# The end of a differential attention: filler products in one wait, short products in two groups, two output columns moved forward

## The chip, the cores and the metric

One core of a Trainium2 chip (trn2) runs the whole program in one launch. The time is device microseconds of an execution, the median of several. Everything below is about one stretch of some 60 us out of 1887.

## The reference

The program computes two transformer blocks over 512 tokens of width 1024. The stretch at hand is the last attention, `diff_attention`: 8 heads, each the difference of two softmaxes, then a norm over each head's 128 values, then the output projection, added to the residual.

```python
s = einsum('bhitd,bhisd->bhits', q, k) * scale      # two score maps per head
s = s + bias; s = where(dist >= 0, s, -inf)
p = softmax(s, axis=-1)
a = p[:, :, 0] - lam * p[:, :, 1]
o = einsum('bhts,bhsd->bhtd', a, v)                 # 8 heads x 128 values per token
o = rms_norm_2(o, subln) * (1.0 - lambda_init)      # norm over the 128 values of one head
x = x + o.reshape(B, S, V_WIDTH) @ w_o              # 1024 -> 1024
```

## The kernel before, in words

Every dense product is made of three TensorE products of rounded halves: high by high, low by high, high by low (lines 475 to 477). ScalarE rounds a weight unit to its high half (`w_hi`, line 1126), VectorE subtracts to get the low half (`w_lo`, line 1693), and SyncE's queue loads the next raw unit when VectorE has finished with the slot. There are two weight slots.

The attention is a software pipeline of items. Item n stands for head n//4 and query block n%4, so there are 32 items, and each engine has its own function `diff_item(n)` that is called for n = 0, 1, 2, ... in order. Each engine works strictly down its own list; semaphores (`a3[...]`) join them. In call n TensorE does, in this order: `turn(n-4)`, transposes of the finished probabilities against `ident` (line 1028); `scores(n)`, six products over 64 rows (line 1017); now and then `head_sums`, the sums of squares of one finished head (line 972, a column of ones as the moving operand); `heads_turned` and `head_spread`, which turn four heads' factors into rows and spread them over 128 partitions with products over only 4 rows (lines 980, 990, 991); half of a query/key panel (up to call 25); and in odd calls `weigh(n-6)`, probabilities by values. VectorE does in call n: the low half of the turned probabilities (line 2370) for n-5, `inverse(n-2)`, `least(n)` (line 2345, which waits for the scores), `probs(n-3)` (line 2361, for which the turn waits), weight low halves (line 1693), and `head_normed` and `head_lo` for heads whose factors are there (lines 2421 and 2426). ScalarE does the exponentials, the high halves and the copy of a finished head out of bank 6 (line 1610), and `head_square` (line 1651).

The output projection is cut in two. Heads 0 to 3 give the "early" part: 8 columns (j = 0 to 7) of 128 output channels, each a chain of 12 products of 512 columns (`early_column`), in banks 7 and 3 by turns, each added to `x` by VectorE (line 1756) before the bank is used again. Two columns share a weight unit, and a unit's slot is free after the second. Heads 4 to 7 give the "bo" part behind all of that (`into_residual`), whose first column goes head by head and waits for each head's low half (`a3["out_lo"]`).

In the kernel before, early columns 0 to 3 stand in calls 30, 31, 33 and 35, and columns 4 to 7 behind the loop, between the last sums of squares, the turned factors and the four spreads of heads 4 to 7. `output_column(0)` waits for all four heads 0 to 3.

Of the kernel before, what the change touches and what calls it, by code (L numbers as in the profile page):

```python
# [122 lines left out]
def bass_two_blocks(nc, weights, x_cols, mem_cols, positions, params, consts, dil_table, head_rows, alibi_table, head_picks,  # L123
# [26 lines left out]
    with ctx:  # L150
# [156 lines left out]
            return [half.rearrange("p (j b n) -> p j b n", b=2, n=P) for half in halves]  # L307

        BO_EARLY = 4 * N_DIFF - 2
        COLUMN_ITEMS = (BO_EARLY, BO_EARLY + 1, BO_EARLY + 3, BO_EARLY + 5)  # L310

        def head_squares(h):

# [79 lines left out]
        OPENING_BANKS = (0, 1, 4, 5, 6)  # L393
        OPENING = len(OPENING_BANKS)
        IDLE_PRODUCTS = 13

        ROWS = {"mix": 0, "first": 1, "a": 2, "kv": 3}

# [73 lines left out]
        def _(pe):  # L472
# [494 lines left out]
            def head_sums(h):  # L967

                pe.wait_ge(a3["sq"], h + 1)
                for b in range(TB):  # L970
                    i = 16 * (h // 4) + TB * b + h % 4
                    mm = nc.tensor.matmul(ps[:, 2, i:i + 1], head_squares(h)[:, b, :], ones[:, 0:1], start=True, stop=True)  # L972
                mm.then_inc(a3["summed"], 1)
# [9 lines left out]
            def head_spread(h, bank):  # L983

                g = h // 4
                if h % 4 == 0:
                    pe.wait_ge(a3["rms"], 4 * g + 5)
                hi, lo = token_rows(g)
                pick = head_picks_r[:, h % 4 * P:(h % 4 + 1) * P]
                nc.tensor.matmul(ps[:, bank, :], pick, hi, start=True, stop=False)  # L990
                nc.tensor.matmul(ps[:, bank, :], pick, lo, start=False, stop=True).then_inc(a3["spread"], 1)

            def output_column(j):

                if j == 0:
                    pe.wait_ge(a3["out_lo"], 4)
                if j < 2:
                    pe.wait_ge(a3["normed"], 3 + j)
                else:
                    pe.wait_ge(early["added"], ADDED["bo_early"] + j - 1)  # L1000
                early_column("bo_early", j, 3 if j % 2 else 7, da["xb_hi"], da["xb_lo"])

            def diff_item(n):
                def scores(n):
                    s, b = n // TB, n % TB
                    if b == 0:
                        pe.wait_ge(a3["staged"], 2 * (s + 1))
                    if n:
                        pe.wait_ge(a3["least"], 2 * n)
                    w = P * (b + 1)  # L1010
                    qh, ql, kh, kl = (at3[f"{p}{s % 2}"] for p in ("qhi", "qlo", "khi", "klo"))
                    block_ = slice(b * P, (b + 1) * P)

                    for k, (q_, k_) in enumerate(((qh, kh), (qh, kl), (ql, kh))):
                        for h in range(2):
                            rows = slice(HD * h, HD * h + HD)
                            mm = nc.tensor.matmul(ps[:, h, 0:w], q_[rows, block_], k_[rows, 0:w],  # L1017
                                                  start=k == 0, stop=k == 2)
                            if k == 2:
                                mm.then_inc(a3["scores"], 1)  # L1020

                def turn(n):
                    b = n % TB
                    pe.wait_ge(a3["probs"], n + 1)
                    if n >= 2:
                        pe.wait_ge(a3["pt"], n - 1)
                    for j in range(b + 1):
                        mm = nc.tensor.transpose(ps[:, 4 + n % 2, j * P:(j + 1) * P],  # L1028
                                                 at3["e"][:, 2 * (n % DIFF_SLOTS), j * P:(j + 1) * P], ident)
                    mm.then_inc(a3["turned"], 1)  # L1030

                def weigh(n):
                    s, pair = n // TB, n % TB // 2
                    pe.wait_ge(a3["pt"], n + 1)
                    if pair == 0:
                        pe.wait_ge(a3["v_staged"], s + 1)
                        pe.wait_ge(a3["out"], s + 1)
                    vh, vl = at3[f"vhi{s % 2}"], at3[f"vlo{s % 2}"]
                    hi, lo = turned_pair(s, pair)
                    last = 2 * pair + 1  # L1040
                    for j in range(last + 1):
                        cols = slice(j * P, (j + 1) * P)
                        one = j == last
                        mm = product(ps[:, 6, (2 * pair + one) * P:2 * (pair + 1) * P].rearrange("p (b n) -> p b n", n=P), vh[:, cols], vl[:, cols],
                                     hi[:, j, one:, :], lo[:, j, one:, :], j == 0, j == last)
                    mm.then_inc(a3["pv"], 1)

                if live(n - 4):
                    turn(n - 4)
                if live(n):  # L1050
                    scores(n)
                if n >= 12 and n % TB == 0 and n // TB - 3 < N_DIFF - 1:
                    head_sums(n // TB - 3)
                if n == 25:
                    heads_turned(0, 3)
                if n == 26:
                    pe.wait_ge(kv["qk"], 2 * N_DIFF)
                    head_spread(0, 7)
                if n == 27:
                    head_spread(1, 3)  # L1060
                    pe.wait_ge(a3["normed"], 1)
                    head_spread(2, 7)
                if n == 28:
                    pe.wait_ge(a3["normed"], 2)
                    head_spread(3, 3)
                p = EARLY_PANELS + n // 2
                if p < 2 * N_DIFF:

                    if n % 2 == 0 and n:
                        pe.wait_ge(kv["qk"], p)  # L1070
                    half_panel(qk0 + p, ps[:, 7, :], *qk_input(p), n % 2)
                if n in COLUMN_ITEMS:
                    output_column(COLUMN_ITEMS.index(n))
                if live(n - 6) and n % 2:
                    weigh(n - 6)

            diff_items(diff_item, 6)
            pe.wait_ge(a3["least"], 8 * N_DIFF)
            output_column(4)
            head_sums(N_DIFF - 1)  # L1080
            output_column(5)
            heads_turned(1, 0)
            output_column(6)
            for h, bank in ((4, 1), (5, 2), (6, 0), (7, 1)):
                if h == 7:
                    pe.wait_ge(a3["normed"], 5)
                head_spread(h, bank)
            output_column(7)
            into_residual("bo", KC, 4, da["xb_hi"], da["xb_lo"], a3["out_lo"], lambda k: k + 1,
                          {0: (a3["pt"], 4 * N_DIFF), 2: (a3["out"], N_DIFF + 1), 3: (early["added"], ADDED["bo_early"] + KC - 1),  # L1090
                           4: (a3["normed"], N_DIFF), 7: (early["added"], ADDED["bo_early"] + KC)}, LAST)
# [26 lines left out]
        def _(act):  # L1118
            def split(u, i=None):

                if u >= N_UNITS:
                    return
                act.wait_ge(w_loaded[u % 2], at(16 * (u // 2 + 1), i, 16))
                if u >= 2:
                    act.wait_ge(used, at(u - 1, i, 2))
                nc.scalar.activation(w_hi[:, u % 2, :], w_raw[:, u % 2, :], ACT.Copy).then_inc(w_hi_ready, 1)  # L1126
# [455 lines left out]
            def diff_item(n):  # L1582
# [56 lines left out]
                    head_hi(2)  # L1639
                if n == 29:  # L1640
                    head_hi(3)
                for f in (0, 1):
                    if n == COLUMN_ITEMS[2 * f + 1] + 1:
                        split(FIRST["bo_early"] + 2 + f)

            def head_square(h):
                act.wait_ge(a3["v_staged"], 1 + h % 2)
# [39 lines left out]
        def _(dve):  # L1687
# [644 lines left out]
            def diff_item(n):  # L2332
# [60 lines left out]
                    head_normed(2, 7)  # L2393
                    head_lo(0)
                if n == 28:
                    head_normed(3, 3)
                    head_lo(1)
                    head_lo(2)
                if n == 29:
                    head_lo(3)  # L2400
                if n - 1 in COLUMN_ITEMS:
                    output_column(COLUMN_ITEMS.index(n - 1))
                for f in (0, 1):
                    if n == COLUMN_ITEMS[2 * f + 1] + 1:
                        split(FIRST["bo_early"] + 2 + f)

            def heads_inverse(g):

# [10 lines left out]
            def head_normed(h, bank):  # L2419
                dve.wait_ge(a3["spread"], 5 * (h // 4) + h % 4 + 2)  # L2420
                nc.vector.scalar_tensor_tensor(out=da["o"][:, h, :], in0=da["o"][:, h, :], scalar=subln[:, 0:1],
                                               in1=ps[:, bank, :], op0=ALU.mult, op1=ALU.mult).then_inc(a3["normed"], 1)
# [7 lines left out]
                early_sum("bo_early", j, 3 if j % 2 else 7)  # L2430

            diff_items(diff_item, 5)
            output_column(4)
            heads_inverse(1)
            output_column(5)
            heads_lo(1)
# [2 lines left out]
            head_normed(4, 1)  # L2439
            head_normed(5, 2)  # L2440
            head_lo(4)
            head_normed(6, 0)
            head_lo(5)
            head_normed(7, 1)
            head_lo(6)
            output_column(7)
            head_lo(7)
            split(FIRST["bo"] + 1)
            dve.wait_ge(early["added"], ADDED["bo_early"] + KC)
# [309 lines left out]
```

## Time and profile before

| | us |
|---|---|
| median of 3 runs (1888.59, 1888.62, 1890.22) | 1888.62 |
| the profiled execution's own time | 1889.28 |
| its span, first to last instruction | 1887.4 |
| TensorE busy in that span | 1863.0 (99%) |
| VectorE busy | 1098.3 (58%) |
| ScalarE busy | 768.0 (41%) |

The span is what the trace shows; 1.9 us of the execution lie around it. The mean granted TensorE clock is 0.992 of full speed. The page's strip of 40 slices has the granted clock at 9 tenths or more in all but two slices (one in the attention's end, one at the end of the program). A stretch of the trace is read from the window view, which gives the busy time of each engine in it and the granted clock.

### The profile page before, as it was taken

Reading aid. Unit: us, or ns where it says so; the run is one execution under the profiler, and the core shown is the slowest. Engines: PE = TensorE matmul, PEld = TensorE weight load, DVE = VectorE, ACT = ScalarE, POOL = GpSimd, SP = SyncE. Lnnn points to the kernel's source line nnn. Section 1 sums busy time; section 2 is a strip of 40 time slices with the busy share of each in tenths; the row PEclk is TensorE's granted clock in tenths of the full one; section 3 lists DMA queues with packets and bytes.
Section 4 is the critical chain, followed back from the end, with each engine's and each line's share of the span. In section 5 each row is a group of like instructions: output and inputs, shape, how many; then the busy total and the mean of one; then the engine's idle time right before and its main releaser. Section 6 shows DMA issues by size and latency. Waiting matters only on the chain.

```text
span 1887.4 us, 24931 instructions
## 1 busy us (share of the span) xinstructions
PE 1863.0 (99%) x8782; PEld 1526.1 (81%) x8782; DVE 1098.3 (58%) x1577; ACT 768.0 (41%) x1182; POOL 261.1 (14%) x206
## 2 busy tenths in 40 slices
PE   9999999999999999999999999999999999999998
PEld 7877888788888888888888888888787888888886
DVE  6867976676777524677544442254888654444223
ACT  4226654355545413563333222144557433323212
POOL 4803320020000001301100000021643110000001
PEclk9999999999999999999999999999998999999998
DMA  5232322122222332222222322332211222222232
GB/s 181 92 109 73 103 97 76 56 90 100 90 99 89 123 100 89 93 87 90 98 97 95 98 95 96 100 104 96 68 56 34 68 95 96 98 97 95 97 100 78
DMA packets 62837, 174.48 MB, mean 92 GB/s; under 512 B 5428, under 2 KB 23988, under 8 KB 62648
## 3 DMA queue, kind: packets, MB, share of 16 engines
q1 hardware_dynamic: 61424, 169.50, 26.8%
q10 hardware_dynamic: 1016, 2.92, 0.5%
q0 software_dynamic: 336, 1.25, 0.2%
q8 instruction: 39, 0.64, 0.1%
q14 instruction: 22, 0.18, 0.0%
HBM read 171.54 MB, written 2.10 MB: 92 GB/s over the span
## 4 chain that ended last, share of the span: by engine, by line
PE 91%; DVE 6%; ACT 1%; issue 1%; DMA 0%; POOL 0%; SPq 0%; POOLq 0%; DVEq 0%; ACTq 0%
PE ps L475 29%; PE ps L477 29%; PE ps L476 29%; DVE w_lo L1693 1%; PE ps L1017 1%; PE ps L1028 1%; DMA x<-in_x_cols 0%; PE ps L972 0%; DVE at_e L1928 0%; DVE sg_z L2225 0%; ACT w_hi L1126 0%; PE ps L503 0%; DVE sg_t L2221 0%; PE ps L685 0%; DVE sg_u L2230 0%
## 5 line engine op out<-in xcount | busy, mean ns | idle before, releaser
L1693 DVE TENSOR_TENSOR w_lo<-w_raw,w_hi 128x1024 fp32r<-128x1024 f32 x314 | 405.5, 1291 | 456.4 <-ACT w_hi L1126 455.9
L475 PE MATMUL ps<-xg_hi,w_hi 128*128 128x512 f32 (+1 forms) x1448 | 564.7, 390 | 4.2 <-DVE w_lo L1765 1.9
L476 PE MATMUL ps<-xg_lo,w_hi 128*128 128x512 f32 (+1 forms) x1448 | 557.6, 385 | 0.0
L477 PE MATMUL ps<-xg_hi,w_lo 128*128 128x512 f32 (+1 forms) x1448 | 557.3, 385 | 0.0
L1126 ACT ACTIVATE w_hi<-w_raw 128x1024 fp32r<-128x1024 f32 x314 | 330.5, 1052 | 533.7 <-PE ps L477 529.7
L475 PEld LDWEIGHTS ps<-xg_hi,w_hi 128*128 128x128 f32 x1448 | 272.3, 188 | 70.9 <-DVE w_lo L1693 7.8
L477 PEld LDWEIGHTS ps<-xg_hi,w_lo 128*128 128x128 f32 x1448 | 272.4, 188 | 54.7
L476 PEld LDWEIGHTS ps<-xg_lo,w_hi 128*128 128x128 f32 x1448 | 272.6, 188 | 53.3 <-issue 1.0
L475 PE MATMUL ps<-hid_hi,w_hi 128*128 (+1 forms) x528 | 205.5, 389 | 0.0
L477 PE MATMUL ps<-hid_hi,w_lo 128*128 (+1 forms) x528 | 205.4, 389 | 0.0
L476 PE MATMUL ps<-hid_lo,w_hi 128*128 (+1 forms) x528 | 205.4, 389 | 0.0
L2476 POOL COPY square_sum<-squares 128x512 f32<-128x512 f32 x7 | 4.8, 686 | 947.0 <-ACT squares L1141 946.0
L475 PEld LDWEIGHTS ps<-hid_hi,w_hi 128*128 128x128 f32 x528 | 99.1, 188 | 20.9 <-DVE w_lo L1693 0.4
L476 PEld LDWEIGHTS ps<-hid_lo,w_hi 128*128 128x128 f32 x528 | 99.1, 188 | 20.7
L477 PEld LDWEIGHTS ps<-hid_hi,w_lo 128*128 128x128 f32 x528 | 99.1, 188 | 20.4
L2479 POOL TENSOR_TENSOR square_sum<-square_sum,squares 128x512 f32<-128x512 f32 x49 | 78.3, 1597 | 61.3 <-ACT squares L1141 60.3
L475 PE MATMUL ps<-w_hi,xg_hi 128*128 128x512 f32 x192 | 77.4, 403 | 0.3 <-DVE w_lo L1693 0.3
L1714 DVE TENSOR_TENSOR conv_a<-ps,r_cols 128x512 f32<-128x512 f32 x44 | 30.4, 691 | 78.5 <-PE ps L477 78.5
L477 PE MATMUL ps<-w_hi,xg_lo 128*128 128x512 f32 x192 | 74.8, 390 | 0.0
L476 PE MATMUL ps<-w_lo,xg_hi 128*128 128x512 f32 x192 | 74.8, 390 | 0.0
L1543 ACT ACTIVATE gate<-conv_g 128x512 f32<-128x512 f32 x44 | 27.8, 632 | 109.0 <-DVE conv_g L1714 109.0
L1699 DVE SCALAR_TENSOR_TENSOR xg_lo<-x,par,xg_hi 128x512 fp32r<-128x512 f32 x56 | 60.7, 1098 | 6.7 <-ACT xg_hi L1191 6.6
(375 smaller groups left out, 2460.6 us busy)
## 6 DMA issues: line engine op xcount, KB each, us to landing
w_raw<-in_weights SPq DMA_DIRECT2D x315, 512.0 KB, 3.3
out_cols<-result SPq DMA_DIRECT2D x8, 256.0 KB, 2.2
x<-in_x_cols SPq DMA_DIRECT2D x2, 512.0 KB, 5.7
x<-in_x_cols SPq DMA_DIRECT2D x1, 1024.0 KB, 8.9
squares<-in_mem_cols ACTq DMA_DIRECT2D x1, 512.0 KB
sp_w<-in_spatial ACTq DMA_DIRECT2D x1, 512.0 KB
sp_b<-in_spatial_bias ACTq DMA_DIRECT2D x1, 512.0 KB
dil<-in_dil_table POOLq DMA_DIRECT2D x1, 448.0 KB, 4.8
```

The source lines that it names most:

```text
L475: nc.tensor.matmul(to, wh, xh, start=start, stop=False)
L476: nc.tensor.matmul(to, wh, xl, start=False, stop=False)
L477: return nc.tensor.matmul(to, wl, xh, start=False, stop=stop)
L1017: mm = nc.tensor.matmul(ps[:, h, 0:w], q_[rows, block_], k_[rows, 0:w], start=k == 0, stop=k == 2)
L1028: mm = nc.tensor.transpose(ps[:, 4 + n % 2, j * P:(j + 1) * P], at3["e"][:, 2 * (n % DIFF_SLOTS), j * P:(j + 1) * P], ident)
L1126: nc.scalar.activation(w_hi[:, u % 2, :], w_raw[:, u % 2, :], ACT.Copy).then_inc(w_hi_ready, 1)
L1543: nc.scalar.activation(ffn["gate"][:], ffn["tg"][:], ACT.Silu).then_inc(st["gated"], 1)
L1693: nc.vector.tensor_tensor(w_lo[:, u % 2, :], w_raw[:, u % 2, :], w_hi[:, u % 2, :].bitcast(F32), ALU.subtract).then_inc(w_ready, 1)
L1699: nc.vector.scalar_tensor_tensor(out=xg_lo[:, c, :], in0=x[:, c, :], scalar=column(gain, c), in1=xg_hi[:, c, :].bitcast(F32), op0=ALU.mult ...
L1714: return nc.vector.tensor_tensor(to, ps[:, bank, 0:cols], r_cols[:] if r is None else r, ALU.mult).then_inc(signal, 1)
L2476: nc.gpsimd.tensor_copy(sums[:], squares[:, 0, :]).then_inc(summed, 1)
L2479: nc.gpsimd.tensor_tensor(sums[:], sums[:], squares[:, c % 2, :], ALU.add).then_inc(summed, 1)
```

## The change

On TensorE, `turn(23)` (IDLE_TURN) gets eight products of `ident` by `ident` between its two waits: after the wait for the bank, ahead of the wait for the probabilities. Columns 0 and 1 of the early part leave calls 30 and 31; `first_columns(h)` does the share of head h in both columns at once (six products), in call 28 (h = 0), 29 (h = 1 and 2) and 30 (h = 3). Columns 2, 3 and 4 go to calls 32, 33 and 35, so one column fewer stands behind the loop. `head_spread(3)` goes to bank 2 and no longer waits for `normed` 2; `head_sums(4)`, which uses bank 2 too, goes from call 28 to call 30. Behind the loop the four spreads are done as 4 and 5, then column 7, then 6 and 7. ScalarE and VectorE follow: columns 0 and 1 are both added in call 31, weight units 2 and 3 of the early part are split in calls 31 and 34 (before: 32 and 36), column 4 is added in call 36, and column 7 ahead of `head_normed(6)`.

```diff
-        COLUMN_ITEMS = (BO_EARLY, BO_EARLY + 1, BO_EARLY + 3, BO_EARLY + 5)
+        COLUMN_ITEMS = (BO_EARLY + 2, BO_EARLY + 3, BO_EARLY + 5)
+        IDLE_TURN = 4 * N_DIFF - 9
+            def first_columns(h):
+                u = FIRST["bo_early"]
+                if h == 0:
+                    pe.wait_ge(w_ready, u + 1)
+                    pe.wait_ge(a3["normed"], 3)
+                pe.wait_ge(a3["out_lo"], h + 1)
+                for j in range(2):
+                    wh, wl = tile(u % 2, 2 * h + j)
+                    mm = product(ps[:, 3 if j else 7, :], wh, wl, da["xb_hi"][:, h, :], da["xb_lo"][:, h, :], h == 0, h == LAST - 1)
+                    if h == LAST - 1:
+                        mm.then_inc(used if j else early["first"], 1)
...
-                    pe.wait_ge(a3["probs"], n + 1)
                     if n >= 2:
                         pe.wait_ge(a3["pt"], n - 1)
+                    if n == IDLE_TURN:
+                        for _ in range(8):
+                            nc.tensor.matmul(ps[:, 4 + n % 2, 0:P], ident, ident, start=True, stop=True)
+                    pe.wait_ge(a3["probs"], n + 1)
...
-                if n >= 12 and n % TB == 0 and n // TB - 3 < N_DIFF - 1:
+                if n >= 12 and n % TB == 0 and n // TB - 3 < N_DIFF - 1 and n != 28:
                     head_sums(n // TB - 3)
+                if n == 30:
+                    pe.wait_ge(a3["normed"], 4)
+                    head_sums(4)
...
                 if n == 28:
-                    pe.wait_ge(a3["normed"], 2)
-                    head_spread(3, 3)
+                    head_spread(3, 2)
...
+                if n == 28:
+                    first_columns(0)
+                if n == 29:
+                    first_columns(1)
+                    first_columns(2)
+                if n == 30:
+                    first_columns(3)
 
             diff_items(diff_item, 6)
             pe.wait_ge(a3["least"], 8 * N_DIFF)
-            output_column(4)
             head_sums(N_DIFF - 1)
             output_column(5)
             heads_turned(1, 0)
             output_column(6)
-            for h, bank in ((4, 1), (5, 2), (6, 0), (7, 1)):
-                if h == 7:
-                    pe.wait_ge(a3["normed"], 5)
-                head_spread(h, bank)
+            head_spread(4, 1)
+            head_spread(5, 2)
             output_column(7)
+            head_spread(6, 0)
+            pe.wait_ge(a3["normed"], 5)
+            head_spread(7, 1)
```

## Rows read from the trace of the kernel before

**Rows 1.** The page: busy us of each engine and share of the span.
```profile
PE 1863.0 (99%) x8782; PEld 1526.1 (81%) x8782; DVE 1098.3 (58%) x1577; ACT 768.0 (41%) x1182; POOL 261.1 (14%) x206
```

**Rows 2.** Windows: length; PE, PEld, DVE, ACT, POOL busy (count); clock; DMA; GB/s.
```profile
1439.42:1453.06 13.64, 13.64 (x58) 9.93 (x54) 12.56 (x36) 8.20 (x21) 0.75 (x2) 0.50 0.12 40
1487.20:1490.62 3.42, 3.42 (x10) 2.65 (x9) 2.07 (x4) 1.26 (x2) 0.00 (x0) 0.50 0.00 0
1453.06:1487.20 34.14, 34.14 (x191) 27.68 (x192) 20.41 (x42) 17.16 (x35) 1.72 (x2) 1.00 0.15 47
```

**Rows 3.** Timeline of TensorE, calls 26 to 29: start, us, operation, count [idle before].
```profile
1434.80 0.52 PE L1028 MATMUL ps<-con,at_e 128*128 128x128 f32 x3
1435.97 0.49 PE L990 MATMUL ps<-xg_hi 4*128 4x512 f32 x1
1438.47 0.66 PE L1028 MATMUL ps<-con,at_e 128*128 128x128 f32 x4 [1.78 <-DVE at_e L2361]
1446.84 0.79 PE L990 MATMUL ps<-xg_hi 4*128 4x512 f32 x1
1447.98 0.69 PE L1028 MATMUL ps<-con,at_e 128*128 128x128 f32 x2
1449.54 0.58 PE L475 MATMUL ps<-at_pt_hi,at_v_hi 128*128 128x256 f32 x1
```

**Rows 4.** Timeline of VectorE, calls 27 to 31.
```profile
1443.22 0.35 DVE L2361 SCALAR_TENSOR_TENSOR at_e<-at_e,at_inv 128x128 f32<-128x128 f32 x1
1444.80 0.68 DVE L2426 TENSOR_TENSOR xb_lo<-da_o,xb_hi 128x512 fp32r<-128x512 f32 x1
1446.77 0.48 DVE L2361 SCALAR_TENSOR_TENSOR at_e<-at_e,at_inv 128x256 f32<-128x256 f32 x1
1459.45 0.35 DVE L2361 SCALAR_TENSOR_TENSOR at_e<-at_e,at_inv 128x128 f32<-128x128 f32 x1
```

**Rows 5.** Timeline of TensorE, calls 31 to 36 and the six steps behind the loop.
```profile
1456.58 0.60 PE L1028 MATMUL ps<-con,at_e 128*128 128x128 f32 x4
1461.52 0.29 PE L1028 MATMUL ps<-con,at_e 128*128 128x128 f32 x1
1471.91 0.36 PE L475 MATMUL ps<-at_pt_hi,at_v_hi 128*128 128x256 f32 x1
1473.35 0.44 PE L475 MATMUL ps<-xb_hi,w_hi 128*128 128x512 f32 x1
1476.16 0.95 PE L972 MATMUL ps<-con,da_v 128*128 128x1 f32 x8
1483.86 0.49 PE L990 MATMUL ps<-xg_hi 4*128 4x512 f32 x1
1486.08 0.50 PE L475 MATMUL ps<-xb_hi,w_hi 128*128 128x512 f32 x1
1488.27 0.63 PE L476 MATMUL ps<-xb_lo,w_hi 128*128 128x512 f32 x1
1488.69 0.63 PE L477 MATMUL ps<-xb_hi,w_lo 128*128 128x512 f32 x1
1490.40 0.49 PE L475 MATMUL ps<-xb_hi,w_hi 128*128 128x512 f32 x1
```

**Rows 6.** Timeline of ScalarE behind the last weigh.
```profile
1474.22 0.63 ACT L1651 ACTIVATE da_v<-da_o 128x512 f32<-128x512 f32 x1
```

**Rows 7.** Timeline of TensorE at the start; two windows of it.
```profile
1.19 5.36 PE L594 MATMUL ps<-squares 128*128 128x128 f32 x26 [1.19 <-DVE squares L1759]
5.80:6.55 0.75, 0.75 (x7) 0.55 (x5) 0.00 (x0) 0.72 (x1) 0.00 (x0) 1.00 0.95 382
9.26:12.68 3.42, 3.42 (x9) 2.35 (x9) 2.22 (x4) 2.29 (x4) 0.92 (x2) 0.51 1.00 379
```

**Rows 8.** Two thin windows of the first attention.
```profile
162.90:166.40 3.50, 2.12 (x17) 1.84 (x18) 1.97 (x3) 3.45 (x10) 2.22 (x4) 1.00 0.00 0
197.00:200.50 3.50, 2.60 (x28) 2.18 (x27) 3.43 (x10) 1.30 (x4) 0.00 (x0) 1.00 0.27 90
```

More of the change, by code:

```diff
@@ L991, in head_spread @@
                 nc.tensor.matmul(ps[:, bank, :], pick, lo, start=False, stop=True).then_inc(a3["spread"], 1)
-            def output_column(j):
[L995 to L1000, printed above, removed]
+            def first_columns(h):
[9 more added lines that the diff above has]
+                        mm.then_inc(used if j else early["first"], 1)
+            def output_column(j):
+                pe.wait_ge(early["added"], ADDED["bo_early"] + j - 1)
                 early_column("bo_early", j, 3 if j % 2 else 7, da["xb_hi"], da["xb_lo"])
@@ L1072, in diff_item @@
                 if n in COLUMN_ITEMS:
-                    output_column(COLUMN_ITEMS.index(n))
+                    output_column(2 + COLUMN_ITEMS.index(n))
                 if live(n - 6) and n % 2:
                     weigh(n - 6)
+                if n == 28:
[5 more added lines that the diff above has]
+                    first_columns(3)
             diff_items(diff_item, 6)
             pe.wait_ge(a3["least"], 8 * N_DIFF)
-            output_column(4)
             head_sums(N_DIFF - 1)
@@ L1641, in diff_item @@
                     head_hi(3)
-                for f in (0, 1):
-                    if n == COLUMN_ITEMS[2 * f + 1] + 1:
-                        split(FIRST["bo_early"] + 2 + f)
+                if n == BO_EARLY + 1:
+                    split(FIRST["bo_early"] + 2)
+                if n == COLUMN_ITEMS[1] + 1:
+                    split(FIRST["bo_early"] + 3)
             def head_square(h):
@@ L2395, in diff_item @@
                 if n == 28:
-                    head_normed(3, 3)
+                    head_normed(3, 2)
                     head_lo(1)
@@ L2400, in diff_item @@
                     head_lo(3)
+                if n == BO_EARLY + 1:
+                    output_column(0)
+                    output_column(1)
                 if n - 1 in COLUMN_ITEMS:
[L2402 to L2405, printed above, removed]
+                    output_column(2 + COLUMN_ITEMS.index(n - 1))
+                if n == BO_EARLY + 1:
+                    split(FIRST["bo_early"] + 2)
+                if n == COLUMN_ITEMS[1] + 1:
+                    split(FIRST["bo_early"] + 3)
             def heads_inverse(g):
@@ L2432, in _ @@
             diff_items(diff_item, 5)
-            output_column(4)
             heads_inverse(1)
@@ L2441, in _ @@
             head_lo(4)
+            head_lo(5)
+            output_column(7)
             head_normed(6, 0)
-            head_lo(5)
             head_normed(7, 1)
             head_lo(6)
-            output_column(7)
             head_lo(7)
```

## The prediction, made before the changed kernel was seen

> **What bounds the kernel now.** I read the page first: TensorE is busy for 1863.0 us, 99% of the span [rows 1]. So an edit pays only by work taken off TensorE, by a gap closed, or by TensorE running at its higher clock. No product is taken away here; one gap is filled. The window view shows the third: in 13.64 us of the stretch the granted clock is 0.50, that is 1.2 GHz, and again in 3.42 us behind it; the 34.14 us between are at 1.00, 2.4 GHz [rows 2]. The timeline of TensorE shows what goes ahead of each fall: a spread over 4 rows, 1.78 us in which it waits for VectorE's `probs(23)`, four transposes and products over 64 rows [rows 3]; and, in the second place, the four spreads over 4 rows, 1483.86 to 1486.08 [rows 5]. These are the two places that the change touches. The third view is VectorE in the same 13.64 us: 12.56 us busy [rows 2]. The low clock is therefore not all that TensorE pays there. Even at full clock it would stand behind VectorE.
>
> The sum is made against the profiled execution, 1889.28 us (span 1887.4 and 1.9 around it), and is then moved to the median of 1888.62, which lies 0.66 lower.
>
> **The identity products.** Eight products of an f32 operand. The thirteen f32 products of the same size at the program's start have 26 records, so each is two passes and eight are 16. Those 26 took 5.36 us, 0.21 each; the last seven, in 0.75 us, 0.11 to 0.13 each [rows 7]. Sixteen cost 1.7 to 2.0 us at the fast pitch and 3.4 at the slow one. The wait is 1.78 us, so `turn(23)` starts 0 to 0.3 us later, or 1.6 later at the slow pitch. Either is hidden: the next thing TensorE needs from VectorE is `probs(24)`, which ends at 1443.22 + 0.35 = 1443.57 [rows 4], and VectorE comes to it through its own queue (the weight unit, one norm, the two maps of call 27). Cost taken: 0. Without that cover it would be 0.3.
>
> **Do they hold the clock?** Through the wait, I think yes. But what follows is thin as well, and stays thin at full clock: scores over 64 rows, spread 1, a wait for `normed` 1, spread 2, six products of `weigh(21)`, a wait until 1443.57 for `probs(24)`, one transpose, small scores, spread 3, and then a wait for `out_lo` 1, which is written at 1444.80 + 0.68 = 1445.48 [rows 4]. The changed call 28 has dense work only from there on. So I take it that the fall is put off, not gone: half rate from about 1442.8, and the high clock back at about 1449.7, behind the first six column products. The two ends for this are no low stretch at all, and one that lasts to 1453.06 as before.
>
> **Calls 28 to 31, walked through.** VectorE's order does not change up to `probs(25)`, whose end is 1446.77 + 0.48 = 1447.25 [rows 4]. In the middle case:
> - `turn(24)` and `scores(28)`, then spread 3 at half rate, done at about 1445.7. Spread 3 comes some 2 us earlier than before (it began at 1446.84 and took 1.0 [rows 3]) because the sums of head 4 are gone from ahead of it.
> - Six column products at 0.425 (1488.27 to 1488.69 is one at half rate [rows 5]), 2.55: 1448.3.
> - `turn(25)` and `scores(29)` at half rate, 1447.98 to 1449.54, 1.56 [rows 3]: 1449.85.
> - `weigh(23)`: twelve products at full rate, 1471.91 to 1473.35, 1.44 [rows 5]: 1451.3.
> - Heads 1 and 2, twelve products, 2.81 (column 4: 1473.35 to 1476.16 [rows 5]): 1454.1.
> - `turn(26)` and `scores(30)`, as 1434.80 to 1435.97, 1.17 [rows 3]: 1455.3; the sums of head 4, about 0.9 (0.95 for such a group at 1476.16 [rows 5]): 1456.2; head 3, 1.4: 1457.6.
> - `turn(27)` to the end of `probs(28)`: before, 1456.58 [rows 5] to 1459.45 + 0.35 [rows 4], 3.2. It is a chain over scores, VectorE's two minima and `probs`, and TensorE has only the scores and `weigh(25)` to put beside it, 2.1 us; so it now stands idle for 1.1. `turn(28)` at 1460.8, and before at 1461.52 [rows 5].
>
> This part gives -0.7 us: the move fills what VectorE made thin, but one column of cover (2.8) is gone from call 31. Of what is queued behind the waiting `first_columns` on TensorE only `turn(25)` matters, and that has its own wait until 1447.25. The units' splits at calls 31 and 34 come earlier than their users (columns 4 to 7); SyncE's loads follow those splits and have several us in hand: 0.
>
> With no low stretch at all the same walk gives `turn(28)` at about 1459.0, -2.5. With a low one up to 1453.06 it adds 1.6: +0.9.
>
> **Behind call 31.** Columns 2, 3 and 4 are now inside the loop, the same work in another order: 0. But before, column 4 (2.8 us) lay between `weigh(31)` and the sums of head 7. Those sums need head 7 copied and squared, and the square ended at 1474.22 + 0.63 = 1474.85 [rows 6], 1.5 us behind the end of `weigh(31)` at 1473.35 [rows 5]. Nothing covers that chain now: +1.5.
>
> **Two groups of spreads.** Column 7 took 1486.08 to 1490.40, 4.32, against 2.81 at full rate [rows 5]. With 1.1 us of spreads, a dense column and 1.1 us again I expect no fall: -1.5. The low end of this is 0 (it falls all the same).
>
> **VectorE behind column 7.** It adds column 7 (0.7), norms heads 6 and 7, and takes both low halves, one at a time with 0.6 to 0.7 each. The low half of head 6 is there some 2.8 us behind column 7; TensorE comes to it after two spreads (1.1) and the six products of heads 4 and 5 (1.4), so it waits for 0.3: +0.3. Bounds 0 and 1.
>
> **Sum.** -0.7 + 1.5 - 1.5 + 0.3 = -0.4 us, 1888.9 for the profiled execution and 1888.2 for the median.
>
> **A rule weighed.** Rows first: the clock is at 0.50 for 13.64 + 3.42 = 17.06 us [rows 2]. The Trainium skill, "TensorE: Matmul & The Clock Gate", section "Terms", puts the penalty of throttled time at that time by (1 - K/N), half of it here. By that the change could win 8.5 us, where I count 2.5 + 1.5 at best before the new gaps.
>
> **Rivals.**
> - *The clock's half comes back whole.* 13.64 / 2 + 1.5 = 8.3 us, less the new waits of 1.5 and 0.3 and a part of the 1.1: -6, 1882.6. For it: TensorE had no gap in the 13.64 us. Against it: VectorE is 92% busy there, and `probs(24)` and `probs(25)` don't come earlier. Chance 0.12. The rule of the skill above is this case.
> - *No low stretch, but VectorE as counted.* -2.5 + 1.5 - 1.5 + 0.3 = -2.2, 1886.4. For it: windows of the first attention in which TensorE was busy for only 2.12 and 2.60 of 3.50 us kept 1.00 [rows 8]. Against it: they held dense products, and the thin stretch here holds few. Chance 0.14.
> - *The other side: the new gap behind `weigh(31)` brings the clock down.* There 1.5 us of idle and 0.9 of products with one column follow 1.4 us of dense ones. The rows decide neither way: a window with about as little, 197.00 to 200.50, kept 1.00 [rows 8], and at the program's start, less than 3 us behind the last pass of the f32 products, the clock was 0.51 [rows 7]. If it falls as the second stretch of before did, 3.42 us at half rate under the sums and column 5 cost 1.7: sum +1.3, 1889.9. It decides from the clock in column 5. Chance 0.25.
> - *The identity products don't help:* the low stretch lasts to about 1453 as before. Sum -0.4 + 1.6 = +1.2, 1889.8. Chance 0.13; together with the one before, 1891.5 and more, within these two.
> - *The forecast,* one shorter low stretch and none later, 0.36.
>
> **How the numbers follow.** A measurement of this kernel can tell about 0.2%, 3.8 us, from no change. Faster by more: the first rival, and a part of the second if VectorE gives more than I count, 0.16. Slower by more needs both falls and a third in the gap of call 32, 0.07. Within: 0.77. The forecast is 1888.2; alone its range is 1887.2 to 1889.2. The whole range takes in the second rival and both falls, and leaves most of the first outside: 1884.8 to 1891.4.
>
> **What would show it.** The gap before `turn(23)` filled with 16 passes of `ident` (0.12 each) and `turn(23)` within 0.3 us of its place. Granted clock 1.00 to about 1442.8 and 0.50 for some 7 us. A wait of TensorE for VectorE's line 2361 in call 32 of about 1.1 us, one for ScalarE's `head_square` of 1.5 us before the last sums. Column 7 in 2.8 us. I am wrong if VectorE's busy time in calls 27 to 31 turns out to have been stretched by TensorE's low clock, or if the clock falls where I have it high.

## The result: 4.1 us slower, and the profile after

The changed kernel takes 1892.91 us (median of 17; 1892.05 to 1894.45), the kernel before 1888.83 (median of 17; 1888.35 to 1890.22). The ratio is 1.0020, 95% interval [1.0013, 1.0027]. The forecast was 1888.2 with a range up to 1891.4, so the time lies outside it, on the slow side.

The profiled execution took 1892.56 us, span 1890.7. First the page: engine, busy us, share, instructions. Against [rows 1] TensorE has 16 more instructions, 3.0 us more busy time and 2.3 us more of weight loads (PEld). The other engines stay within 0.3 us.

```profile
PE 1866.0 (99%) x8798; PEld 1528.4 (81%) x8798; DVE 1098.2 (58%) x1577; ACT 768.3 (41%) x1182; POOL 261.3 (14%) x206
```

Then the windows with a granted clock below 1.00 in the attention's end (columns as in [rows 2]):

```profile
1443.54:1450.26 6.72, 6.72 (x27) 4.71 (x24) 6.12 (x21) 5.20 (x15) 0.00 (x0) 0.50 0.01 2
1477.60:1484.41 6.81, 6.81 (x21) 4.95 (x21) 0.79 (x2) 1.42 (x3) 0.00 (x0) 0.50 0.00 0
1484.41:1495.03 10.62, 10.45 (x45) 7.05 (x43) 8.19 (x13) 3.83 (x7) 0.00 (x0) 1.00 0.16 51
```

The first low stretch has gone from 13.64 us to 6.72. The one of 3.42 under column 7 is gone. But there is a new one of 6.81 us, in a place where the kernel before had 1.00. The timeline of TensorE (start, us, operation, count, [idle before <- releaser]) shows what lies around both:

```profile
1435.24 0.49 PE L991 MATMUL ps<-xg_hi 4*128 4x512 f32 x1
1435.90 2.05 PE L1037 MATMUL ps<-con 128*128 128x128 f32 x16
1437.79 0.62 PE L1040 MATMUL ps<-con,at_e 128*128 128x128 f32 x4
...
1442.99 0.30 PE L1040 MATMUL ps<-con,at_e 128*128 128x128 f32 x1 [0.80 <-DVE at_e L2383]
...
1445.01 0.80 PE L476 MATMUL ps<-xb_hi,w_hi 128*128 128x512 f32 x1
...
1447.73 0.63 PE L1040 MATMUL ps<-con,at_e 128*128 128x128 f32 x2
...
1449.23 0.58 PE L476 MATMUL ps<-at_pt_hi,at_v_hi 128*128 128x256 f32 x1
...
1460.83 0.30 PE L1040 MATMUL ps<-con,at_e 128*128 128x128 f32 x1 [1.03 <-DVE at_e L2383]
...
1477.11 1.40 PE L973 MATMUL ps<-con,da_v 128*128 128x1 f32 x8 [1.49 <-ACT da_v L1673]
1478.37 0.77 PE L476 MATMUL ps<-xb_hi,w_hi 128*128 128x512 f32 x1
1478.94 0.63 PE L477 MATMUL ps<-xb_lo,w_hi 128*128 128x512 f32 x1
...
1483.77 1.34 PE L981 MATMUL ps<-con,lam_in 128*4 128x128 f32 x8
1485.04 0.50 PE L476 MATMUL ps<-xb_hi,w_hi 128*128 128x512 f32 x1
...
1489.12 0.50 PE L476 MATMUL ps<-xb_hi,w_hi 128*128 128x512 f32 x1
...
1493.19 0.50 PE L476 MATMUL ps<-xb_hi,w_hi 128*128 128x512 f32 x1
...
1495.03 0.50 PE L476 MATMUL ps<-xb_hi,w_hi 128*128 128x512 f32 x1 [0.17 <-DVE xb_lo L2452]
```

In the kernel before, column 6 starts here:

```profile
1480.89 0.50 PE L475 MATMUL ps<-xb_hi,w_hi 128*128 128x512 f32 x1
```

The two executions are laid on each other at spread 0 (1435.24 here, 1435.97 in [rows 3]), so 0.73 is added to the times here. That 0.73 is also why the two profiled executions differ by only 3.28 us (1892.56 less 1889.28): up to spread 0 both kernels do the same work, and this execution happened to be there earlier. Then `turn(28)` is at 1461.56 against 1461.52 [rows 5]: nothing won. The last sums are at 1477.84 against 1476.16: 1.7 lost. Column 6 is at 1485.77 against 1480.89: 4.9 lost. The "bo" part starts at 1493.92 (1493.19 above) against 1490.40 [rows 5]: 3.5 lost, and 0.3 more where its third head waits. The whole loss arises between `weigh(31)` and column 6: 1.7 us of wait and 3.2 us of half clock, of which the two groups of spreads give 1.4 back.

### The profile page after: what moved, and what is told of

The parts are those of the page before. It is cut to its first block, busy times and chain, and to the rows that moved or that the text cites. A ratio compares the mean times of both kernels' runs of the same rounds, so it can differ in the third digit from the quotient of the medians.

```text
span 1890.7 us, 24964 instructions
## 1 busy us (share of the span) xinstructions
PE 1866.0 (99%) x8798; PEld 1528.4 (81%) x8798; DVE 1098.2 (58%) x1577; ACT 768.3 (41%) x1182; POOL 261.3 (14%) x206
## 4 chain that ended last, share of the span: by engine, by line
PE 91%; DVE 6%; issue 1%; ACT 1%; DMA 0%; POOL 0%; SPq 0%; POOLq 0%; DVEq 0%; ACTq 0%
PE ps L476 29%; PE ps L477 29%; PE ps L478 29%; DVE w_lo L1715 1%; PE ps L1026 1%; PE ps L1040 0%; DMA x<-in_x_cols 0%; PE ps L973 0%; PE ps L686 0%; DVE at_e L1950 0%; DVE sg_z L2247 0%; PE ps L504 0%; DVE sg_t L2243 0%; PE ps L695 0%; DVE sg_u L2252 0%
```

## The experiments

All times are medians, beside runs of the kernel before on the same chip (1889.13 for the first four, 1889.3 for the next four, 1889.18 for the last four). In the result it was 1888.83, so the same kernel differs by 0.3 to 0.5 us from one set of runs to the next, and a difference between kernels of different sets is not known better than that. The two numbers in brackets behind a ratio are its 95% interval.

**1. Column 4 put back behind the loop.**

```diff
-        COLUMN_ITEMS = (BO_EARLY + 2, BO_EARLY + 3, BO_EARLY + 5)
+        COLUMN_ITEMS = (BO_EARLY + 2, BO_EARLY + 3)
...
+            output_column(4)
             head_sums(N_DIFF - 1)
```

VectorE adds column 4 behind the loop as well (left out above).

> The changed kernel with early column 4 put back behind the loop, between weigh(31) and the sums of head 7. Theory A (the loss sits in the uncovered chain behind weigh(31): 1.5 us of gap, and a low clock of 6.8 us under the sums, column 5 and the turned factors that costs 3.4): about 4.9 us less than the changed kernel, 1888.0, no wait before the last sums, clock 1.00 there. Theory B (the loss sits in calls 28 to 31, where the two columns are gathered head by head and call 31 has lost its cover): at most 0.5 us less, 1892.4 or more.

Measured 1892.4 (1890.82 to 1894.45), ratio to before 1.0017 [1.0008, 1.0026]. By its number this is theory B's result, but the trace doesn't put the loss in calls 28 to 31:

```profile
1469.46 0.95 PE L1040 MATMUL ps<-con,at_e 128*128 128x128 f32 x7
1472.15 1.05 PE L973 MATMUL ps<-con,da_v 128*128 128x1 f32 x8 [0.87 <-ACT da_v L1674]
1473.58 0.39 PE L476 MATMUL ps<-at_pt_hi,at_v_hi 128*128 128x256 f32 x1 [0.37 <-DVE at_pt_lo L2393]
```

and, its windows there:

```profile
1469.00:1475.10 6.10, 4.85 (x40) 4.43 (x40) 2.29 (x3) 2.93 (x5) 0.00 (x0) 1.00 0.22 73
1475.13:1478.54 3.41, 3.41 (x10) 2.64 (x10) 0.00 (x0) 2.51 (x3) 0.00 (x0) 0.50 0.06 20
```

The wait before the last sums is covered again, and two waits have opened in calls 36 and 37, where column 4 had been the cover; the clock falls behind them instead. My reading is that the two columns done early leave one too few for the waits behind call 31, wherever it is missing; theory A then had the mechanism and the wrong remedy, for its 1888.0 was missed by 4.4.

**2. The wait before the last sums filled.** Six products of `ident` by `ident` into bank 0, just ahead of `head_sums(N_DIFF - 1)`:

```diff
             pe.wait_ge(a3["least"], 8 * N_DIFF)
+            for _ in range(6):
+                nc.tensor.matmul(ps[:, 0, 0:P], ident, ident, start=True, stop=True)
             head_sums(N_DIFF - 1)
```

> The changed kernel with six more products of the identity (12 passes, about 1.45 us) in the gap before the sums of head 7; the gap itself stays. Theory A with the clock as its larger part: clock 1.00 in column 5, about 3.4 us less than the changed kernel, 1889.5. If the gap alone is the price: 1892.9, no change. If the identity's products don't count for the clock: 0.50 in column 5 all the same, and 1892.9 to 1893.1.

Measured 1889.88 (1889.32 to 1891.25), ratio 1.0005 [0.9996, 1.0014]: 3.0 us less than the changed kernel, although 12 instructions were added and TensorE still waits for head 7's squares. (Each taken against the kernel before of its own set, the difference is 3.3.) Its highest time, 1891.25, lies below the changed kernel's lowest, 1892.05. The timeline and one window:

```profile
1475.40 1.55 PE L1101 MATMUL ps<-con 128*128 128x128 f32 x12
1476.96 1.05 PE L973 MATMUL ps<-con,da_v 128*128 128x1 f32 x8
1477.88 0.48 PE L476 MATMUL ps<-xb_hi,w_hi 128*128 128x512 f32 x1
```

```profile
1476.00:1484.40 8.40, 8.39 (x48) 6.61 (x47) 2.76 (x4) 3.92 (x6) 0.00 (x0) 1.00 0.00 0
```

The "bo" part starts 54.64 us behind spread 0 here and 57.95 in the changed kernel, 3.3 apart. This is the cause of most of the loss, shown: the low clock behind the wait, not the wait. What is left above the kernel before, 0.75, agrees with the wait's 1.7, the two groups' -1.4 and the 0.3 of the third head.

**3. Without the products of the identity.** The loop of eight in `turn(23)` left out.

> The changed kernel without its eight products of the identity in turn(23). My walk: the clock falls some 3.4 us earlier, but TensorE stands behind VectorE's probs(24) and probs(25) there, so it costs 0 to 0.5 us: 1892.9 to 1893.4. Rival (the products hold the clock and that is worth what the low stretch costs): 1.7 us or more, 1894.6 and up. Third: they only delay turn(23), and without them it is up to 0.3 us faster.

Measured 1893.2 (1892.54 to 1894.95), 1.0023 [1.0014, 1.0033]: 0.3 more than the changed kernel, and equal to it (4.1 each) when each is taken against the kernel before of its own set. Both lie within my walk's 0 to 0.5. The first low stretch is 10.24 us long, from 1440.10, instead of 6.72, and that costs almost nothing: `turn(28)` is 25.64 us behind spread 0, in the changed kernel 25.59.

```profile
1440.10:1450.34 10.24, 9.89 (x34) 6.46 (x33) 9.16 (x28) 7.03 (x18) 0.00 (x0) 0.51 0.17 53
```

**4. The four spreads together again**, in the changed kernel: spreads 4, 5, 6, 7, then column 7, VectorE's order as before.

> The changed kernel with the four spreads of heads 4 to 7 together again, column 7 behind them and VectorE's order as before the change. If the grouping is worth what I gave it (1.5 us of column 7 at half rate, less 0.3 of waiting on VectorE): 1.2 us more, 1894.1, clock 0.50 in column 7. Rival (the fall there depends on what else is thin nearby and does not come every time): between -0.3 and 0, 1892.6 to 1892.9.

Measured 1893.82 (1890.57 to 1895.12), 1.0021 [1.0012, 1.0030], but the 11 times lie in two heaps, five from 1890.57 to 1891.62 and six from 1893.82 to 1895.12. The profiled execution is in the lower one, with 3.41 us at 0.50 behind the wait (1478.11 to 1481.52) where the changed kernel had 6.81. And its column 7 ran at 1.00, although the four spreads stood together before it:

```profile
1482.00:1496.00 14.00, 14.00 (x63) 10.32 (x63) 10.80 (x15) 5.46 (x8) 0.00 (x0) 1.00 0.14 43
```

The grouping is worth 0.6 to 0.9 here by the medians, below my 1.2. With two heaps that figure depends on how many executions fall into each, and which falls the upper heap has is not shown, since none of it was profiled.

**5. The grouping alone**, in the kernel before (the `for` over four spreads replaced by the order of the change, on VectorE too).

> The kernel before with only the grouping of the four spreads (4 and 5, column 7, 6 and 7, and VectorE's order with it). The grouping is worth what I predicted: clock 1.00 in column 7, -1.5 + 0.3 = -1.2 us, 1887.9. Rival: the fall there comes at another place or not in every execution, so that little is left: 1888.8 to 1889.4.

Measured 1888.97 (1887.87 to 1890.09), 0.9997 [0.9988, 1.0006]. Its trace has 1.00 throughout column 7 and "bo" starts 52.99 us behind spread 0 where the kernel before needed 54.43, 1.4 of the 1.5 I had predicted; by the medians only 0.3 is left. The number is the rival's. That the fall under column 7 is not in every execution of the kernel before is an inference: with the four spreads together, experiments 4 and 9 each have a trace without it.

**6. The columns' move alone**: the changed kernel without the eight products and with the spreads together.

> The changed kernel without the products of the identity and with the spreads together: what is left is the gathering of columns 0 and 1 in calls 28 to 30 and one column fewer behind the loop. Theory (the columns' move is what costs; the rest is small): 4 to 5.5 us more than before, 1893.2 to 1894.6, with the 1.5 us wait before the last sums and a low clock behind it. Rival (the parts hurt only together): below 1891.

Measured 1894.19 (1891.64 to 1895.30), 1.0024 [1.0015, 1.0033], 4.9 us above before, as the theory had it. Its trace has the wait of 1.49 us before the last sums and this behind it:

```profile
1477.50:1484.32 6.82, 6.82 (x21) 5.20 (x21) 0.25 (x1) 1.25 (x2) 0.00 (x0) 0.50 0.00 0
```

The move is the part that costs; the other two soften it by 0.8 (each against before of its own set) to 1.3.

**7. Every wait filled**, in the changed kernel: 3 products ahead of `pe.wait_ge(a3["normed"], 1)`, in `turn` this, 3 ahead of the first `out_lo` wait, and the six of experiment 2.

```diff
-                    if n == IDLE_TURN:
-                        for _ in range(8):
+                    if n in (23, 24, 25, 28):
+                        for _ in range({23: 8, 24: 3, 25: 1, 28: 4}[n]):
```

The other three places (left out above) are loops like experiment 2's.

> The changed kernel with products of the identity in every wait of TensorE from call 27 on: 8 in turn(23) as there, 3 before spread 2, 3 and 1 and 4 in turn(24), turn(25) and turn(28), 3 before the first column products, 6 before the last sums. Two theories on what the low clock of calls 28 and 29 is worth. VectorE sets the order there: the clock stays at 1.00, turn(25) still starts only behind probs(25), and it is 2 to 2.5 us faster than with the last sums' gap filled alone (1889.9): 1887.5. The clock's half comes back whole: 3.4 us (half of 6.9) faster, 1886.5 or less. If the filler takes time itself: 1889.9 or more.

Measured 1888.7 (1887.43 to 1890.49), 0.9996 [0.9987, 1.0005]: 1.2 us less than experiment 2, where I had expected 2 to 2.5. In the traces the "bo" part comes 2.1 earlier (52.54 us behind spread 0 against 54.64), so the medians give back less than this one execution shows. One window over calls 27 to 31:

```profile
1436.00:1460.00 24.00, 24.00 (x160) 18.99 (x160) 22.30 (x56) 17.97 (x46) 5.78 (x5) 1.00 0.07 23
```

and around `probs(25)`, VectorE's line 2389, TensorE's turn:

```profile
1446.68 0.48 DVE L2389 SCALAR_TENSOR_TENSOR at_e<-at_e,at_inv 128x256 f32<-128x256 f32 x1
```

```profile
1435.87 0.49 PE L991 MATMUL ps<-xg_hi 4*128 4x512 f32 x1
1447.30 0.38 PE L1042 MATMUL ps<-con,at_e 128*128 128x128 f32 x2
1459.24 0.33 PE L1042 MATMUL ps<-con,at_e 128*128 128x128 f32 x1
```

The clock never falls, TensorE has no gap, and `turn(25)` still starts only behind `probs(25)`. `turn(28)` comes 23.37 us behind spread 0, where the kernel before had 25.55 (1461.52 less 1435.97) and the changed kernel 25.59: 2.2 us. Against the changed kernel, which has the same products in the same order, that is 2.2 for 6.72 us of low clock, not 3.4. The rival that the half comes back whole asked for 1886.5 or less; no time is below 1887.43.

**8. The kernel before, waits filled, spreads in two groups.** 8, 3, 6 and 4 products in `turn(23)` to `turn(26)`, 3 ahead of spread 2.

> The kernel before, columns where they were, with products of the identity in the waits of calls 27 to 30 (8 in turn(23), 3 before spread 2, then 3, 6 and 4 in turn(24) to turn(26)) and the spreads in two groups. VectorE as the limit: the clock stays at 1.00, turn(26) starts some 1.2 us earlier, and with 1.2 from the grouping it is 1886.7. If half of the 13.64 us comes back: 1882. If the filler only delays the turns: 1889 or more.

Measured 1888.45 (1887.57 to 1889.41), 0.9994 [0.9985, 1.0003]. Less than I expected (1886.7). In its trace the clock fell all the same, at 1447.0, half a microsecond after the twelve passes in `turn(25)` had begun. They took 2.44 us, and the turn started 1.1 us behind the end of `probs(25)` (1447.53):

```profile
1446.42 2.44 PE L1028 MATMUL ps<-con 128*128 128x128 f32 x12
1448.65 0.63 PE L1031 MATMUL ps<-con,at_e 128*128 128x128 f32 x2
```

**9. Column 4 forward, in the kernel before**, the one edit that bares the last wait and leaves calls 28 to 31 alone.

```diff
+                if n == 36:
+                    output_column(4)
                 if live(n - 6) and n % 2:
                     weigh(n - 6)
...
-            output_column(4)
             head_sums(N_DIFF - 1)
```

> The kernel before with one edit: early column 4 is done in call 36, ahead of weigh(31), and no longer between weigh(31) and the sums of head 7. The work is the same. Theory (the cover of the chain behind weigh(31) is the loss, and calls 28 to 31 have no part in it): a wait of 1.5 us before the last sums, 0.50 in column 5, and 3 to 5 us more than before, 1892.3 to 1894.3. Rival (it takes the thin calls of the changed kernel as well): at most 1.5 us more, 1890.8.

Measured 1892.12 (1888.61 to 1892.74), 1.0015 [1.0006, 1.0024]: 2.9 above before. Eight of the 11 times lie from 1891.43 to 1892.74, three from 1888.61 to 1889.07. The profiled execution is one of the three. It has the wait, 1.49 us, and no fall behind it:

```profile
1476.97 1.02 PE L972 MATMUL ps<-con,da_v 128*128 128x1 f32 x8 [1.49 <-ACT da_v L1652]
1477.85 0.48 PE L475 MATMUL ps<-xb_hi,w_hi 128*128 128x512 f32 x1
```

```profile
1474.00:1480.00 6.00, 4.51 (x30) 4.03 (x29) 0.94 (x2) 2.78 (x4) 0.00 (x0) 1.00 0.16 56
```

Nor does it have a fall under column 7, with the four spreads together: the 1.5 us of wait and the 1.5 us that column 7 lost in the kernel before cancel, and "bo" starts 54.56 us behind spread 0 against 54.43. So without any move into calls 28 to 30 the bared wait brings 2.9 of the 4.1 us by the medians. Which fall the eight slower ones have, behind the wait or under column 7, is not shown: none of them was profiled.

**10. The same with six products in the wait.**

> The same edit with six products of the identity in the wait before the last sums. The wait stays, the clock should not fall behind it: 1.5 us more than before, 1890.8, and some 3 us less than without the filler. If the clock is not what the wait costs, it equals the run without filler.

Measured 1891.35 (1888.37 to 1893.48), 1.0008 [0.9999, 1.0017]. Only 0.8 less than without, where I expected some 3. Again there are two heaps, five times from 1888.37 to 1889.34 and six from 1891.35 to 1893.48; the profiled execution (1891.73) is in the upper one. Its trace has 1.00 behind the wait, and 0.50 behind the four spreads, under column 7, just where the kernel before has it [rows 2]:

```profile
1487.94 0.62 PE L475 MATMUL ps<-xb_hi,w_hi 128*128 128x512 f32 x1
1488.18:1491.60 3.42, 3.42 (x9) 2.63 (x9) 2.95 (x5) 1.63 (x3) 0.00 (x0) 0.50 0.02 8
```

So this execution pays the wait and the old fall, 2.45 us above the profiled one of the kernel before. It also shows that an execution can be in the upper heap with the clock high behind the wait. The pair of experiments 9 and 10 therefore tells little about the clock's price behind the wait; that rests on experiment 2.

**11. and 12. Only column 0 gathered**, three products a head in calls 28 to 30, all other columns where they were, spread 3 in bank 2, sums of head 4 in call 30, spreads in two groups; first without filler, then with it (8, 3 and 4 products in `turn(23)` to `turn(25)`, 3 before spread 2, 3 before the first gathered products).

```diff
+            def first_column(h):
+                u = FIRST["bo_early"]
+                if h == 0:
+                    pe.wait_ge(w_ready, u + 1)
+                    pe.wait_ge(a3["normed"], 3)
+                pe.wait_ge(a3["out_lo"], h + 1)
+                wh, wl = tile(u % 2, 2 * h)
+                mm = product(ps[:, 7, :], wh, wl, da["xb_hi"][:, h, :], da["xb_lo"][:, h, :], h == 0, h == LAST - 1)
+                if h == LAST - 1:
+                    mm.then_inc(early["first"], 1)
...
-                if n in COLUMN_ITEMS:
+                if n in COLUMN_ITEMS and n != BO_EARLY:
...
+                for h in {28: (0,), 29: (1, 2), 30: (3,)}.get(n, ()):
+                    first_column(h)
```

> The kernel before with only column 0 gathered head by head in calls 28 to 30 (three products a head, spread 3 in bank 2, sums of head 4 in call 30), the other columns where they were, and the spreads in two groups; no filler. Each later gap keeps its cover. Theory (the gathering is good as far as it fills what VectorE makes thin, and bad from where it bares a later wait): no wait before the last sums, about 2 us less than before, 1887.3. Rival (products moved under the low clock cost double, so nothing is won): 1889 or more.

> The same with products of the identity in the waits of calls 27 to 29 (8, 3, 3, 3 and 4). If VectorE sets the order up to probs(25) and TensorE is the limit from there on at full clock: turn(28) some 3.5 us earlier than before, 1.2 us from the grouping, 1884.7. If the filler gives no more than it gave to the changed kernel with all waits filled (1.2 us against the last sums' alone): 1886 to 1887.

Measured 1888.04 (1887.36 to 1889.52), 0.9996 [0.9987, 1.0005], and 1887.24 (1886.66 to 1888.72), 0.9991 [0.9982, 1.0000]. Both fall short of what I expected (1887.3; 1884.7, or else 1886 to 1887), and the first can't be told from no change. The second is the fastest kernel of this study, 1.9 us below before and 5.7 below the changed one, at the edge of what can be told from no change. It has all its cover behind call 31 and one window at 1.00 over calls 27 to 31; two short waits for `probs` are left there, the longer before `turn(27)`:

```profile
1454.96 0.63 PE L1045 MATMUL ps<-con,at_e 128*128 128x128 f32 x4 [0.93 <-DVE at_e L2385]
1459.90 0.30 PE L1045 MATMUL ps<-con,at_e 128*128 128x128 f32 x1
```

The two kernels differ in nothing but the filler, and so they price the low clock of these calls. The windows, first without filler, then with it:

```profile
1437.95:1451.59 13.64, 13.64 (x52) 9.77 (x53) 13.27 (x36) 8.31 (x23) 0.95 (x1) 0.50 0.13 40
1436.00:1460.00 24.00, 22.82 (x150) 17.77 (x150) 22.76 (x59) 17.11 (x46) 5.31 (x5) 1.00 0.07 23
```

`turn(28)` stands 25.81 us behind spread 0 without filler (1461.13 less 1435.32) and 24.47 with it (1459.90 less 1435.43): 1.3 us for 13.64 us of low clock, and 0.8 by the medians.

## Why the prediction was wrong, step by step

**What bounds the kernel, and VectorE's part: right.** With the clock high throughout, `turn(25)` still starts only behind `probs(25)`, which comes no earlier (experiment 7), and `turn(28)` is then 2.2 us ahead of the kernel before, where I had counted 2.5.

**The identity products: right.** They took 1.89 us (1435.90 to 1437.79), `turn(23)` started 0.05 later on the common axis, and without them the kernel is 0 to 0.3 slower. Putting off the fall is what they do: it came at 1443.54 + 0.73 = 1444.3, forecast 1442.8, and without them at 1440.4 on the same axis.

**Calls 28 to 31, -0.7: measured 0.0.** The order and the waits came as walked, the 1.03 us before `turn(28)` too. The high clock came back 1.3 us later than I took it (1450.26 + 0.73 = 1451.0, not 1449.7). `turn(25)` and the scores I had at half rate already, so what it changed is `weigh(23)`: the first part ran at half rate, and it took 1.92 (1449.23 to 1451.15), not 1.44. That is 0.5 of the 0.7; the rest is some 0.1 ahead of it and 0.15 between `turn(27)` and `turn(28)`.

**The wait behind weigh(31), +1.5: measured +1.7,** 1.49 of it the wait.

**The step that failed: the clock behind that wait.** The forecast had it high; the fall stood among the rivals at 0.25, priced at 1.7 us for 3.42 us of low clock. It came, and lasted 6.81 us, under the sums, all of column 5 and the turned factors; that cost 3.2 in the trace, and 3.0 to 3.3 by experiment 2. All 17 times of the changed kernel lie at or above 1892.05, so it is no rare case. Two things had misled me. I took the low stretch of column 7 as the length of such a fall. And I took thin windows of the first attention with 1.00 for evidence, when one profile shows one execution: the changed kernel's own profile has 0.50 in just that place.

```profile
163.54:170.25 6.71, 6.13 (x29) 6.17 (x30) 4.88 (x15) 4.68 (x12) 3.42 (x6) 0.50 0.24 78
```

I had also let a known wait of 1.5 us with thin work behind it pass as a gap only, in a change whose first part exists to fill such a gap.

**Two groups, -1.5: measured -1.4 in the traces** (3.5 - 4.9), and -0.3 to -0.9 by the medians of experiments 5 and 4. A likely reason is that the kernel before does not pay for that fall every time.

**VectorE behind column 7, +0.3: right.** The third head's products start at 1495.03, 0.57 behind the product before, where 0.23 is the pitch.

**The sum.** 0.0 + 1.7 + 3.2 - 1.4 + 0.3 = 3.8, with 4.1 measured; the terms I gave were -0.7, 1.5, 0, -1.5 and 0.3. With the fall at its true length my rival would have stood at 1891.6, just outside my range, and at 1892.3 with the first term at 0. Two slips of the prediction show here as well: both falls together gave 1891.5, just above the 1891.4 that I said took them in; and I took 3.8 us for the least difference that can be told, where the interval of this result is about 1.3 us to either side.

**The rule.** "Terms" in "TensorE: Matmul & The Clock Gate" of the Trainium skill counts half of the throttled time. Where TensorE is the limit, in column 5, that fits: 6.81 / 2 = 3.4, measured 3.0 to 3.3. Beside a full VectorE it doesn't. With the same products in the same order, 13.64 us were worth 1.3 (experiments 11 and 12), not 6.8, and 6.72 us were worth 2.2 (experiment 7 against the changed kernel), not 3.4.

## What to carry to other kernels

Dense work that can be put anywhere is cover; count for every wait behind the place it is taken from what still lies over it, and price a bared wait with the clock behind it, not by its length alone: here 1.5 us of wait cost twice as much again. Low clock cost its half only where TensorE set the pace, so look at the other engines in the same stretch before pricing it. And a clock seen high in one profile is one execution's clock; the spread of the times tells whether it is always so.

## What the runs showed that I had not expected

A dozen passes of a product whose result nobody reads, in a wait, made the kernel 3.0 us faster (experiment 2). But they are no free insurance: where the clock fell just after they began, twelve passes took 2.44 us instead of about 1.5 and held up the turn they were to bridge (experiment 8), and eight products in one wait only put the fall off, from 1440.4 to 1444.3 (experiment 3). The same program's executions also fall into two heaps, 2.7 to 3.6 us apart by the heaps' medians (experiments 4, 9 and 10), though nothing in it is different; a single profile shows one of them. With such a kernel one trace explains one heap, and its median can jump between two values.
